# A two-layer decoder trunk on one core: search counts of ScalarE and filling matmuls laid out anew

## The chip, the core and the metric

The kernel runs on one core of a Trainium2 chip. The metric is the device time of one execution in microseconds (us). TensorE does the matmuls, VectorE, ScalarE and GpSimd the element-wise work, SyncE (the SP queue) issues the DMAs. Each engine runs its instructions in the order in which they are written, and waits on semaphores.

## The reference, cut to what matters

Input x is 1024 tokens by 1024 channels in float32. Layer 0 (even) projects x once and feeds two parallel head groups; layer 1 (odd) is a recurrent block that the change leaves alone.

```
proj = h @ even_w_in
score = sum over 8 index heads of w * relu(q_idx . k_idx), causal
_, idx = top_k(score, 256)                      # per query token
A: softmax over the 256 chosen keys (8 heads, relative bias) @ v, times silu(ag)
B: chunked gated linear attention, 4 heads, chunks of 64, head norm, times silu(bg)
x = x + rmsnorm(concat(A, B) @ even_w_out)
```

The 256 chosen keys of a token are found as a threshold on its score: a binary search over the 31 bits of a float, in which each trial counts how many scores lie above the candidate. Query blocks are 128 tokens; blocks 2 to 7 need the search. Block 7 has 1024 keys, block 6 has 896.

## The kernel before, in words

Every float32 product is made of three matmuls (high with high, high with low, low with high part of the operands), so each weight chunk is copied into a high part by ScalarE (`high(c)`) and a low part by GpSimd (`low(c)`), and each result that is used as an operand is split in the same way by ScalarE and VectorE.

**The search.** VectorE counts for blocks 2 to 5, all in one loop of 31 bits. For blocks 7 and 6 (`SIGNED = [7, 6]`, so b = 0 is block 7 and b = 1 is block 6) ScalarE counts: `sum_signs` (L950 to L964) takes the sign of score minus candidate over the row and sums it; `settle_signs` (L660 to L678) on GpSimd turns the count into the next candidate. Each block needs 32 such counts, one after the other. The 64 counts are placed by hand beside other work: `SIGNS_VALUE` in the 24 value tiles (products of 128 tokens by 256 channels for v of both groups), `SIGNS_KEYS` in the eight half-products of queries and keys of group B, `SIGNS_GATES` in the 16 half-products of the gates. In the gates loop ScalarE copies the half-product out (`gst`), takes its sigmoid (`g_sig`), in odd half-products makes `high` of a coming chunk, then runs `keys_out` (`kn`) and `gla_result` of linear attention, and last the counts. Half-products are numbered 0 to 15. TensorE runs, after half-product i, pieces of linear attention: `gla_turn`, `gla_update`, `gla_output`. `gla_output` waits for the `kn` copies of every turn so far, since both use one bank of PSUM; in half-products 4, 9 and 11 a turn stands directly ahead of an output.

**The masks.** After its loop VectorE fixes the ties of blocks 6 and 7 (`settle_ties`), makes the masks of blocks 2 to 7 (`make_mask`), and between them does `gla_mask` and `gla_state` for linear attention.

**Attention.** It runs in steps a = 0 to 33: 4 pairs of heads by 8 query blocks, so step 8p + q does pair p and block q. In step a TensorE does the logits of a (`head_logits`), then, for step a-1, in groups of up to four key blocks: it transposes the probabilities (`turn`), waits until ScalarE has copied them out (`pT`, L1103), and multiplies with v (`weigh`, L1981). Blocks 4 to 7 have two groups. Between the two, quarter pieces of the projections of the pairs (`pair_part`, 6 matmuls each, products (p, f) with f = 0 to 3, four pieces to a product) fill TensorE. `FILLERS` says how many pieces a step has. A finished product is split by ScalarE (`split_pair`, L1086) at the start of the next step, and by VectorE (`low_pair_result`, L1486), after which the next product may start. `head_logits` of a pair's first block waits until products (p, 0) and (p, 1) are split. VectorE adds the mask and bias to the logits (`masked`, L1498, both heads of the pair), which GpSimd prepares (`near_bias`, L770), and ScalarE takes the exponential (`exponent`, L1092). `head_logits` also waits for `masked` of the step before. In steps 4 to 7 GpSimd scales the results of group B, two tiles a step, each pair of tiles loaded and stored by SP in turn.

**The way out.** The output weights (8 chunks `C_WOE` + k) overwrite the projection's input, so `high` of them waits for the last pair product; one chunk a step in steps 26 to 33. SP loads a chunk when the one two before it has its low part. In SP's order the gates of group B (`mixT<-gate_d`, `load_b_gate`) stand among these loads; `gate_b` on VectorE multiplies them in steps 28 to 32, and TensorE's `turn_gla` waits for that.

Of the kernel before, what the change touches and what calls it, by code (L numbers as in the profile page):

```python
# [26 lines left out]
NT = T // P  # L27
KD = D // P
# [20 lines left out]
SIGNED = [7, 6]  # L49
# [36 lines left out]
def build(nc, x, rel_bias, pre_norm, post_norm, even_w_in, even_gate_w2, gate_b2, even_w_out,  # L86
# [185 lines left out]
    C_AV, C_BV, C_BQK, C_AG, C_BG, C_PAIR, C_WOE, C_ODD, C_WOO = 4, 8, 12, 16, 20, 24, 32, 40, 56  # L272
# [50 lines left out]
        return turned, turned + 1, min(turned + 3, 15)  # L323

    SUMMED_BESIDE, DECAYED_BESIDE = (30, 37), (37, 42)
    MASK_BESIDE = (46, 49, 55)
    STATE_BESIDE = (49, 51, 57)
    SIGNS_VALUE = [2, 1] * (3 * NT // 2)
    SIGNS_KEYS = [2, 1, 2, 1, 2, 1, 2, 1]
    SIGNS_GATES = [2] * 6 + [1] * 4 + [0] * 6  # L330

    INDEXED = []
    for n in range(len(QBS) * PAIRS):
# [8 lines left out]
    w_hi, w_lo = sem("w_hi"), sem("w_lo")  # L342
# [99 lines left out]

    parts = [(p, f, part) for p in range(PAIRS) for f in range(4) for part in range(4)][8:]
    FILLERS, ended = [], {}
    for a, count in enumerate([4, 4, 2, 2, 2, 2, 0, 0] * 3 + [4, 4]):
        FILLERS.append(parts[:count])
        for p, f, part in parts[:count]:
            ended[p, f] = a
        parts = parts[count:]

    def filler(a):

# [182 lines left out]
    def _(pool):  # L635
# [17 lines left out]
        settles, steps = itertools.count(), Tally(settle_step)  # L653
# [5 lines left out]

        def settle_signs():  # L660

            j, b = divmod(next(settles), len(SIGNED))
            w, col = (SIGNED[b] + 1) * P, slice(BY_COUNT + b, BY_COUNT + b + 1)
            up_f, up_i, tried_b = bit_up_f[:, b, :], bit_up_i[:, b, :], tried[:, b:b + 1]
            pool.wait_ge(signs_summed[b], j + 1)
            if j == 0:
                pool.wait_ge(bits_made, BITS + 1)
                own(pool.tensor_scalar(rej[:, col], cnt[:, col], float(w - 2 * TOPK + 1), None, ALU.is_gt))
                own(pool.tensor_scalar(side[:, b:b + 1], rej[:, col], -2.0, 1.0, ALU.mult, ALU.add))
                own(pool.tensor_tensor(up_f, bit_f[:, :], side[:, b:b + 1].to_broadcast([P, BITS + 1]), ALU.mult))  # L670
                own(pool.tensor_copy(up_i, up_f))
                pool.tensor_tensor(cand[:, col], up_i[:, 0:1], rej[:, col], ALU.subtract).then_inc(bit_settled[b], 1)  # L672
            else:
                own(pool.tensor_scalar(rej[:, col], cnt[:, col], float(w - 2 * TOPK + 1), up_f[:, j - 1:j], ALU.is_gt, ALU.mult))
# [42 lines left out]
        for i in range(3):  # L717
            for c in (8 + 2 * i, 9 + 2 * i):
                low(c)
            for t in range(NT):  # L720
                for n in range(SIGNS_VALUE[i * NT + t]):
                    settle_signs()

        pool.wait_ge(proj_full, nth_product("bqk", BQK_ORDER[0], 0))
        pool.memset(tri_f[:, :], 0.0).then_inc(pool_step, 1)
# [18 lines left out]
        for i in range(KD):  # L744
            for hf in range(2):
                pool.wait_ge(proj_copied, copy_count("g", C_AG + i, hf))
                pool.tensor_tensor(gst[:, hf, :], gst[:, hf, :], g_sig[:, :], ALU.mult).then_inc(silu_done, 1)
                if hf:
                    low(C_AG + 2 + i)
                for m in range(SIGNS_GATES[2 * i + hf]):  # L750
                    settle_signs()

        def scale_gla(t):
# [28 lines left out]
        for a in range(NW + 2):  # L782
            if a < NW:
                near_bias(a, 1)
            if a + 1 < NW:
                near_first(a + 1)
            if 4 <= a < 8:
                for t in range(2):
                    scale_gla(2 * (a - 4) + t)
            for p in range(1, PAIRS):  # L790
                for j in range(2):
                    if a == ended[p - 1, 2 + j] + 1:
                        low(C_PAIR + 2 * p + j)
            if 26 <= a < 34:
                low(C_WOE + a - 26)
        for t in range(1, NT):
            if t == 2:
                low(C_ODD)
# [22 lines left out]
    def _(act):  # L821
# [128 lines left out]
        def sum_signs():  # L950

            s = next(sums)
            j, b = divmod(s, len(SIGNED))
            qb, col = SIGNED[b], slice(BY_COUNT + b, BY_COUNT + b + 1)
            if s == 0:
                act.wait_ge(cand_zero, 1)
            else:
                act.wait_ge(signs_summed[(s - 1) % len(SIGNED)], (s - 1) // len(SIGNED) + 1)
# [16 lines left out]
            high(c)  # L975
        for t in range(NT):
            values_out("av", 1, t)
            for n in range(SIGNS_VALUE[t]):
                sum_signs()
        for c in (10, 11):  # L980
            high(c)
        for t in range(NT):
            values_out("bv", 0, t)
            for n in range(SIGNS_VALUE[NT + t]):
                sum_signs()
        for c in (12, 13):
            high(c)
        for pr, g_l in ((0, g_a), (1, kdec[:, 1, :])):
# [5 lines left out]
        for t in range(NT):  # L994
            values_out("bv", 1, t)
            if t == 0:
                own(act.activation(g_n0[:, :], g_a[:, :], ACT.Abs))
            if t == 1:
                own(act.activation(g_n1[:, :], kdec[:, 1, :], ACT.Abs))
            if t == 2:  # L1000
                own(act.activation(g_n0[:, :], g_n0[:, :], ACT.Exp, scale=-1.0))
            if t == 3:
                own(act.activation(g_n1[:, :], g_n1[:, :], ACT.Exp, scale=-1.0))
            if t == 4:
                act.activation(g_n0[:, :], g_n0[:, :], ACT.Ln, bias=onet).then_inc(ln_ready, 1)
            if t == 5:
                act.activation(g_n1[:, :], g_n1[:, :], ACT.Ln, bias=onet).then_inc(ln_ready, 1)
            for n in range(SIGNS_VALUE[2 * NT + t]):
                sum_signs()

        def exponents(pr):
            if pr:
# [37 lines left out]
        for i in range(16):  # L1050
            c, hf = C_AG + i // 2, i % 2
            q = nth_product("g", c, hf)
            act.wait_ge(proj_full, q + 1)
            if c > C_AG:
                act.wait_ge(gate_out[hf], 16 * (c - C_AG))
            act.activation(gst[:, hf, :], ps[:, q % 2, :], ACT.Copy)
            if i:
                act.wait_ge(silu_done, i)
            else:
                act.wait_ge(decs_ready, 2)  # L1060
            act.activation(g_sig[:, :], ps[:, q % 2, :], ACT.Sigmoid).then_inc(proj_copied, 1)
            if hf:
                high(c + 2)
            for t in range(NT):
                if i == gla_at(t)[0]:
                    keys_out(t)
            for t in range(NT):
                if i == gla_at(t)[2]:
                    gla_result(t)
            for m in range(SIGNS_GATES[i]):  # L1070
                sum_signs()
        act.wait_ge(o_out, NT)
        act.activation(grms, gssq, ACT.Sqrt, bias=epst, scale=1.0 / B_VAL).then_inc(gla_root, 1)
# [33 lines left out]
        for a in range(NW + 2):  # L1107
            for p, f in ended:
                if ended[p, f] == a - 1:
                    split_pair(p, f)  # L1110
            if 26 <= a < 34:
                high(C_WOE + a - 26)
            groups = blocks_of[a - 1] if 1 <= a <= NW else []
            for i in range(2):
                for g in groups[i:i + 1]:
# [161 lines left out]
    def _(dve):  # L1277
# [50 lines left out]
        n = 0  # L1328
# [205 lines left out]
            dve.wait_ge(b_turned, i + 1)  # L1534
            dve.tensor_tensor(mixT[:, KD // 2 + j, cols], ps[:, 0, :], mixT[:, KD // 2 + j, cols], ALU.mult).then_inc(b_gated, 1)

        gla_mask(3)
        make_mask(2)
        gla_state(3)
        make_mask(3)  # L1540
        gla_mask(4)
        make_mask(4)
        gla_state(4)
        gla_mask(5)
        make_mask(5)
        gla_state(5)
        settle_ties(1)
        make_mask(6)
        gla_mask(6)
        gla_state(6)  # L1550
        settle_ties(0)
        gla_mask(7)
        make_mask(7)
        gla_state(7)
        for f in range(2):
            low_pair_result(0, f)
        for a in range(NW + 3):
# [163 lines left out]
    def _(pe):  # L1721
# [298 lines left out]
                turn_gla(pieces_at(a)[1])  # L2020

        pe.wait_ge(out_done, NW)
        pe.wait_ge(w_lo, C_ODD)

        def out_tile(t, s, mh, ml, woh, wol, lo_done, freed, full):

            if isinstance(t, int) and t == 0:
                pe.wait_ge(ms_first, 1)
            else:
                pe.wait_ge(lo_done, t)  # L2030
            if freed is not None:
                pe.wait_ge(freed, t - 1)
            for hf in range(2):
                cols = slice(hf * HALF, (hf + 1) * HALF)
                for k in range(KD):
                    last = three(ps[:, S_BANK[s] + hf, :], (mh[:, s, k, :], ml[:, s, k, :]), (woh[:, k, cols], wol[:, k, cols]), k, KD)
            last.then_inc(full, 1)

# [141 lines left out]
```

## Time and profile before

| | |
|---|---|
| median of 3 runs | 1041.27 us (1038.85 to 1043.87) |
| profiled execution | 1043.11 us, span 1041.3 us, mean granted clock 0.982 |
| TensorE busy | 982.8 us, 94% of the span |
| VectorE, ScalarE, GpSimd busy | 630.5, 525.8, 331.2 us |
| value tiles / gates / attention | about 150 to 229 / 270 to 390 / 406 to 628 us |

The span is the trace's length; the profiled execution's own time lies 1.8 us above it. Busy time of TensorE includes matmuls that take twice as long at the lower clock. "Idle before" in a row is the time for which the engine stood still ahead of it, and the name behind the arrow is what ended that.

### The profile page before, as it was taken

To read this page: it belongs to the slowest core of one execution; us is meant where nothing else is said; L and a number is where in the kernel's file an instruction comes from. 1 tells how busy PE (TensorE), PEld (TensorE's weight loads), DVE (VectorE), ACT (ScalarE), POOL (GpSimd) and SP (SyncE) were. 2 spreads that over 40 slices of the span, in tenths; PEclk is the share of its full clock that TensorE was granted. 3 is DMA by queue.
4 is the path that set the end of the run, shared out by engine and by line. 5 is a ranking of instruction groups with operands and counts; after the bars stand their busy time and mean duration, and the time that the engine had idled before them with its cause. 6 is when DMAs were issued, how large, how long until landed. Compare 5 with 4: busy or idle time off the path is not lost.

```text
span 1041.3 us, 15136 instructions
## 1 busy us (share of the span) xinstructions
PE 982.8 (94%) x5706; PEld 799.6 (77%) x5706; DVE 630.5 (61%) x1080; ACT 525.8 (50%) x907; POOL 331.2 (32%) x428
## 2 busy tenths in 40 slices
PE   4998999999999899989999888999999999999997
PEld 3887789988877677767676666888888888888885
DVE  5312889959969781445444562665539394889252
ACT  6423677886755334544545463433437272766221
POOL 1310216546645422433131454110412222215200
PEclk8998999999999999999999998999999999999999
DMA  8243102201223323331010444221321111103152
GB/s 258 61 60 63 42 1 62 61 2 29 65 70 101 92 71 101 104 132 51 12 52 31 142 148 146 101 101 60 101 61 42 50 52 41 47 26 104 47 202 81
DMA packets 73919, 80.06 MB, mean 77 GB/s; under 512 B 5192, under 2 KB 58488, under 8 KB 73848
## 3 DMA queue, kind: packets, MB, share of 16 engines
q1 hardware_dynamic: 72576, 77.49, 23.7%
q10 hardware_dynamic: 1272, 1.62, 1.3%
q8 instruction: 44, 0.72, 0.3%
q14 instruction: 27, 0.22, 0.1%
HBM read 60.23 MB, written 18.35 MB: 75 GB/s over the span
## 4 chain that ended last, share of the span: by engine, by line
PE 67%; DVE 3%; ACT 3%; issue 2%; DMA 2%; POOL 1%; ACTq 0%; POOLq 0%; DVEq 0%
PE ps L1732 19%; PE ps L1734 19%; PE ps L1733 19%; PE ps L1981 3%; PE ps L1965 2%; PE ps L1917 1%; ACT pT L1103 1%; PE ps L1824 1%; DMA g_two<-gla_d 1%; ACT qkH L1086 1%; DVE qkL L1486 1%; PE ps L1912 1%; DMA gla_d<-g_two 1%; PE ps L2044 1%; PE ps L1825 1%
## 5 line engine op out<-in xcount | busy, mean ns | idle before, releaser
L1732 PE MATMUL ps<-hH,wH 128*128 128x512 f32 x384 | 157.3, 410 | 4.5 <-DVE qkL L1486 4.5
L1733 PE MATMUL ps<-hL,wH 128*128 128x512 f32 x384 | 151.2, 394 | 0.0
L1734 PE MATMUL ps<-hH,wL 128*128 128x512 f32 x384 | 151.1, 394 | 0.0
L1732 PE MATMUL ps<-h1H,w_slot_H 128*128 128x512 f32 x256 | 99.9, 390 | 0.0
L1734 PE MATMUL ps<-h1H,w_slot_L 128*128 128x512 f32 x256 | 99.8, 390 | 0.0
L1733 PE MATMUL ps<-h1L,w_slot_H 128*128 128x512 f32 x256 | 99.7, 390 | 0.0
L650 POOL TENSOR_TENSOR wL<-raw,wH 128x1024 fp32r<-128x1024 f32 x32 | 79.3, 2483 | 63.9 <-ACT wH L846 63.4
L1350 DVE TENSOR_SCALAR_CACHE_REDUCE junk<-score,cand 128x768 bf16<-128x768 f32 (+3 forms) x128 | 96.6, 809 | 1.1
L1732 PEld LDWEIGHTS ps<-hH,wH 128*128 128x128 f32 x384 | 73.0, 190 | 23.7 <-issue 9.9
L1734 PEld LDWEIGHTS ps<-hH,wL 128*128 128x128 f32 x384 | 72.9, 190 | 15.8
L1733 PEld LDWEIGHTS ps<-hL,wH 128*128 128x128 f32 x384 | 73.2, 191 | 13.2
L647 POOL TENSOR_TENSOR w_slot_L<-raw,w_slot_H 128x1024 fp32r<-128x1024 f32 x16 | 41.3, 2582 | 125.0 <-ACT w_slot_H L842 125.0
L1732 PE MATMUL ps<-wH,hH 128*128 128x256 f32 x256 | 76.1, 297 | 2.0 <-ACT bv L946 1.8
L963 ACT ACTIVATE signs<-score,cand 128x1024 bf16<-128x1024 f32 x64 | 70.1, 1095 | 7.1 <-POOL cand L672 4.1
L1733 PE MATMUL ps<-wL,hH 128*128 128x256 f32 x256 | 73.1, 286 | 0.0
L1734 PE MATMUL ps<-wH,hL 128*128 128x256 f32 x256 | 73.0, 285 | 0.0
L1103 ACT ACTIVATE pT<-ps 128x512 f32<-128x512 f32 (+3 forms) x96 | 41.9, 488 | 51.8 <-PE ps L1965 51.8
L1092 ACT ACTIVATE prob<-prob,small 128x128 f32<-128x128 f32 (+7 forms) x64 | 49.7, 777 | 30.1 <-DVE small L1504 30.1
L1498 DVE CUSTOM_DVE_ANT_0 prob<-ps,score 128x384 f32<-128x384 f32 (+5 forms) x48 | 42.7, 890 | 29.9 <-POOL score L770 20.0
L1732 PEld LDWEIGHTS ps<-wH,hH 128*128 128x128 f32 x256 | 49.6, 194 | 10.5 <-issue 10.5
L1734 PEld LDWEIGHTS ps<-h1H,w_slot_L 128*128 128x128 f32 x256 | 48.1, 188 | 10.0
L1733 PEld LDWEIGHTS ps<-h1L,w_slot_H 128*128 128x128 f32 x256 | 48.1, 188 | 9.9
(269 smaller groups left out, 2306.1 us busy)
## 6 DMA issues: line engine op xcount, KB each, us to landing
raw<-in_even_w_in SPq DMA_DIRECT2D x32, 512.0 KB, 4.2
xt<-in_x SPq DMA_DIRECT2D x16, 512.0 KB, 6.5
raw<-in_odd_w_in SPq DMA_DIRECT2D x16, 512.0 KB, 3.9
gate_d<-gst SPq DMA_DIRECT2D x16, 256.0 KB, 2.3
raw_row<-in_even_w_out SPq DMA_DIRECT2D x8, 512.0 KB, 3.3
x_d<-xt SPq DMA_DIRECT2D x8, 512.0 KB, 2.6
raw_row<-in_odd_w_out SPq DMA_DIRECT2D x8, 512.0 KB, 3.2
xt<-x_d SPq DMA_DIRECT2D x8, 512.0 KB, 4.8
```

What stands on the lines that cost most here:

```text
L647: pool.tensor_tensor(w_slot_L[s][:, :, :], raw[:, c % 2, :, :], w_slot_H[s][:, :, :].bitcast(F32), ALU.subtract).then_inc(w_lo, 1)
L650: pool.tensor_tensor(wL[:, s, :, :], raw[:, c % 2, :, :], wH[:, s, :, :].bitcast(F32), ALU.subtract).then_inc(w_lo, 1)
L963: act.activation(signs[:, 0:(qb + 1) * P], score_of(qb), ACT.Sign, bias=cand[:, col].bitcast(F32), scale=-1.0, accum_out=cnt[:, col]).then ...
L1092: act.activation(prob[:, i, 0:w], prob[:, i, 0:w], ACT.Exp, bias=nmx[:, c:c + 1], accum_out=lsum[:, c:c + 1]).then_inc(exp_done[e], 1)
L1103: act.activation(pT[:, e, 0:m * P], ps[:, TURN_BANK[e], 0:m * P], ACT.Copy).then_inc(turn_out, 1)
L1350: return steps(dve.tensor_scalar(junk1[:, j % 2, 0:(qb + 1) * P], score_of(qb), threshold, None, op, ALU.add, accum_out=dst[:, j:j + 1]))
L1498: dve.tensor_tensor_reduce(out=prob[:, i, 0:w].rearrange("p (b w) -> p b w", b=banks), in0=ps[:, b:b + banks, 0:wb], in1=mask_of(qb).rearr ...
L1732: pe.matmul(dst, lH, rH, start=k == 0, stop=False)
L1733: pe.matmul(dst, lH, rL, start=False, stop=False)
L1734: return pe.matmul(dst, lL, rH, start=False, stop=k == nk - 1)
L1965: last = pe.transpose(ps[:, TURN_BANK[e], i * P:(i + 1) * P], prob[:, buffer_of(n, e), (first + i) * P:(first + i + 1) * P], ident[:, :])
L1981: both = [pe.matmul(ps[e * A_DIM:(e + 1) * A_DIM, 7, 0:P], v[:, kb, (2 * p + e) * A_DIM:(2 * p + e + 1) * A_DIM], pT[:, e, i * P:(i + 1) * ...
```

## The change

It moves work and takes none away. Value tiles have one count each, all of block 6. The keys have eight counts of block 6 and four of block 7. The gates have two counts of block 7 in each of half-products 0 to 13, the first directly behind the sigmoid and the second where all stood before. The 16 filling pieces of a pair lie in eight steps. The low parts of the output weights come a step later, two of them in step 32, and TensorE waits for them one at a time. On VectorE one `gla_mask` moves into the search loop, and the ties of block 6 come first, those of block 7 last.

```diff
-    MASK_BESIDE = (46, 49, 55)
+    MASK_BESIDE = (46, 49, 55, 59)
-    SIGNS_VALUE = [2, 1] * (3 * NT // 2)
-    SIGNS_KEYS = [2, 1, 2, 1, 2, 1, 2, 1]
-    SIGNS_GATES = [2] * 6 + [1] * 4 + [0] * 6
+    SIGNS_KEYS = [2, 1] * 4
+    SIGNS_GATES = [2] * 14 + [0] * 2
+    SIGN_ORDER = [1] * (3 * NT) + [1, 0, 1] * 4 + [0] * 28
...
-    for a, count in enumerate([4, 4, 2, 2, 2, 2, 0, 0] * 3 + [4, 4]):
+    for a, count in enumerate([4, 4, 2, 2, 1, 1, 1, 1] + [1, 3, 4, 2, 2, 2, 1, 1] * 2 + [1, 3, 4]):
...
+    WOE_STEP = (27, 28, 29, 30, 31, 32, 32, 33)
...
             act.activation(g_sig[:, :], ps[:, q % 2, :], ACT.Sigmoid).then_inc(proj_copied, 1)
+            if SIGNS_GATES[i] > 1:
+                sum_signs()
             if hf:
                 high(c + 2)
...
-            for m in range(SIGNS_GATES[i]):
+            if SIGNS_GATES[i]:
                 sum_signs()
...
-            if 26 <= a < 34:
-                high(C_WOE + a - 26)
+            for k in range(KD):
+                if a == WOE_STEP[k]:
+                    high(C_WOE + k)
...
-        gla_mask(3)
+        gla_state(3)
         make_mask(2)
-        gla_state(3)
+        settle_ties(1)
+        gla_mask(4)
         make_mask(3)
-        gla_mask(4)
         make_mask(4)
...
-        settle_ties(1)
         make_mask(6)
         gla_mask(6)
         gla_state(6)
+        gla_mask(7)
+        gla_state(7)
         settle_ties(0)
-        gla_mask(7)
         make_mask(7)
-        gla_state(7)
...
-        pe.wait_ge(w_lo, C_ODD)
...
+                    if isinstance(t, int) and t == 0 and hf == 0:
+                        pe.wait_ge(w_lo, C_WOE + k + 1)
```

**Place 1: ScalarE, gate half-product 11.** Before, `g_sig` is followed by the high part of a weight chunk, the copy `kn`, and the results of linear attention:

```order
L1056 ACTIVATE gst<-ps 128x512
L1061 ACTIVATE g_sig<-ps 128x512
L846 ACTIVATE wH<-raw 128x1024
L1035 ACTIVATE kn<-ps 128x256
L1043 ACTIVATE g_st<-ps 128x2x2x128
```

In the changed kernel, whose lines are numbered a few higher:

```order
L1060 ACTIVATE gst<-ps 128x512
L1065 ACTIVATE g_sig<-ps 128x512
L970 ACTIVATE signs,cnt<-score,cand 128x1024
L852 ACTIVATE wH<-raw 128x1024
L1039 ACTIVATE kn<-ps 128x256
L1047 ACTIVATE g_st<-ps 128x2x2x128
```

A count over 1024 keys now stands between `g_sig` and `kn`; so it does in half-products 4 and 9.

**Place 2: ScalarE, steps 7 and 8 of attention.** Before, the exponential of block 7's second head (128x1024) is followed by the copies of the next transposes; the split of a pair product (`qkH`) comes only after step 8:

```order
L1103 ACTIVATE pT<-ps 128x384 x2
L1092 ACTIVATE prob,small<-prob,small 128x1024
L1103 ACTIVATE pT<-ps 128x512 x2
L1092 ACTIVATE prob,small<-prob,small 128x128
L1103 ACTIVATE pT<-ps 128x512 x2
L1092 ACTIVATE prob,small<-prob,small 128x128
L1086 ACTIVATE qkH_118<-ps 128x512
```

Changed:

```order
L1109 ACTIVATE pT<-ps 128x384 x2
L1098 ACTIVATE prob,small<-prob,small 128x1024
L1092 ACTIVATE qkH_118<-ps 128x512
L1109 ACTIVATE pT<-ps 128x512 x2
L1098 ACTIVATE prob,small<-prob,small 128x128
```

The split of product (1, 1), which was done in step 6, stands directly behind that exponential, and the logits of step 8 need its result.

**Place 3: ScalarE, steps 26 to 28.** Before, the first output chunk (`woH`) comes in step 26, whose `pT` copies have 256 columns:

```order
L1086 ACTIVATE qkH_118<-ps 128x512
L829 ACTIVATE woH<-raw_row 128x1024
L1103 ACTIVATE pT<-ps 128x256 x2
L1092 ACTIVATE prob,small<-prob,small 128x384 x2
L829 ACTIVATE woH<-raw_row 128x1024
L1103 ACTIVATE pT<-ps 128x384 x2
```

Changed:

```order
L1109 ACTIVATE pT<-ps 128x256 x2
L1098 ACTIVATE prob,small<-prob,small 128x384 x2
L1092 ACTIVATE qkH_118<-ps 128x512
L835 ACTIVATE woH<-raw_row 128x1024
L1109 ACTIVATE pT<-ps 128x384 x2
L1098 ACTIVATE prob,small<-prob,small 128x512 x2
```

The last pair product and the first output chunk both moved one step later; GpSimd's `woL` moved with them, and SP's loads wait for `woL`.

## Rows read from the trace of the kernel before

**Rows 1.** The page, part 5: value tiles; last, idle before, releaser

```profile
L1732 PE MATMUL ps<-wH,hH 128*128 128x256 f32 x256 | 76.1, 297 | 2.0 <-ACT bv L946 1.8
```

**Rows 2.** The view of waits, TensorE alone: us in total, times, longest

```profile
PE ps L1981 <- ACT pT L1103: 10.9, 20, 0.7
```

**Rows 3.** Timeline of ScalarE, half-products 0 and 11 of the gates: start, us

```profile
277.59 1.14 ACT L963 ACTIVATE signs<-score,cand 128x1024 bf16<-128x1024 f32 x1
...
278.86 1.04 ACT L963 ACTIVATE signs<-score,cand 128x896 bf16<-128x896 f32 x1
...
355.55 0.59 ACT L1061 ACTIVATE g_sig<-ps 128x512 f32<-128x512 f32 x1
...
356.97 0.39 ACT L1035 ACTIVATE kn<-ps 128x256 f32<-128x256 f32 x1
```

**Rows 4.** Timeline of TensorE, first row after each wait for kn

```profile
302.09 0.45 PE L1912 MATMUL ps<-state,bqk 64*64 64x128 f32 x8 [0.68 <-ACT kn L1035]
...
341.19 0.45 PE L1912 MATMUL ps<-state,bqk 64*64 64x128 f32 x8 [0.85 <-ACT kn L1035]
...
357.61 0.45 PE L1912 MATMUL ps<-state,bqk 64*64 64x128 f32 x8 [1.73 <-ACT kn L1035]
```

**Rows 5.** Stretches: busy time of each engine, granted clock, DMA share, GB/s

```profile
355.00:360.00 5.00, 3.27 (x36) 2.48 (x34) 0.00 (x0) 2.30 (x4) 3.57 (x2) 0.93 0.29 79
360.00:365.00 5.00, 5.00 (x18) 4.01 (x17) 4.55 (x14) 1.63 (x9) 0.00 (x0) 0.73 0.44 135
400.00:405.00 5.00, 3.50 (x16) 2.61 (x15) 0.69 (x1) 0.60 (x1) 0.00 (x0) 1.00 0.21 81
```

**Rows 6.** Chain that ended last, steps 7 to 9: start, us, what

```profile
455.91 0.02 ACT prob L1092
...
457.86 0.23 PE ps L1732
...
466.81 0.61 ACT qkH L1086
...
468.28 0.47 PE ps L1732
```

**Rows 7.** Timeline of TensorE: second pair product; logits of step 8

```profile
403.67 0.47 PE L1732 MATMUL ps<-hH,wH 128*128 128x512 f32 x1 [1.50 <-DVE qkL L1486]
...
455.83 0.39 PE L1824 MATMUL ps<-qkH 64*128 64x256 f32 x2 [0.76 <-DVE small L1498]
```

**Rows 8.** Timeline of TensorE in steps 14 to 16

```profile
502.04 0.33 PE L1981 MATMUL ps<-pT,v 128*64 128x128 f32 x2 [0.63 <-ACT pT L1103]
...
504.84 0.50 PE L1824 MATMUL ps<-qkH 64*128 64x512 f32 x2
...
511.60 0.39 PE L1824 MATMUL ps<-qkH 64*128 64x256 f32 x2
```

**Rows 9.** Timeline of ScalarE, last exponential of step 15

```profile
510.63 1.15 ACT L1092 ACTIVATE prob<-prob,small 128x1024 f32<-128x1024 f32 x1
```

**Rows 10.** Timeline of TensorE, logits of steps 27 and 28

```profile
589.32 0.50 PE L1824 MATMUL ps<-qkH 64*128 64x512 f32 x2 [1.00 <-DVE small L1498]
...
593.92 0.42 PE L1824 MATMUL ps<-qkH 64*128 64x320 f32 x2 [1.18 <-DVE small L1498]
```

**Rows 11.** Timeline of GpSimd, low part of the first output chunk

```profile
589.07 2.38 POOL L641 TENSOR_TENSOR woL<-raw_row,woH 128x1024 fp32r<-128x1024 f32 x1
```

**Rows 12.** Timeline of the SP queue, steps 26 to 28

```profile
585.52 0.93 SPq L577 DMA_DIRECT2D g_back<-gla_d  x2
...
595.93 0.33 SPq L473 DMA_DIRECT2D raw_row<-in_even_w_out  x1
...
596.78 0.91 SPq L538 DMA_DIRECT2D mixT<-gate_d  x2
```

**Rows 13.** Timeline of VectorE: a gate of group B; step 32

```profile
602.50 0.69 DVE L1535 TENSOR_TENSOR mixT<-ps,mixT 128x512 f32<-128x512 f32 x1 [0.83 <-DMA mixT<-gate_d]
...
619.89 2.15 DVE L1511 COPY rl<-small 128x128 f32<-128x128 f32 x1
```

More of the change, by code:

```diff
@@ L660, in settle_signs @@
         def settle_signs():
-            j, b = divmod(next(settles), len(SIGNED))
+            s = next(settles)
+            b = SIGN_ORDER[s]
+            j = SIGN_ORDER[:s].count(b)
             w, col = (SIGNED[b] + 1) * P, slice(BY_COUNT + b, BY_COUNT + b + 1)
@@ L720, in _ @@
             for t in range(NT):
-                for n in range(SIGNS_VALUE[i * NT + t]):
-                    settle_signs()
+                settle_signs()
         pool.wait_ge(proj_full, nth_product("bqk", BQK_ORDER[0], 0))
@@ L747, in _ @@
                 pool.tensor_tensor(gst[:, hf, :], gst[:, hf, :], g_sig[:, :], ALU.mult).then_inc(silu_done, 1)
+                if SIGNS_GATES[2 * i + hf] > 1:
+                    settle_signs()
                 if hf:
                     low(C_AG + 2 + i)
-                for m in range(SIGNS_GATES[2 * i + hf]):
+                if SIGNS_GATES[2 * i + hf]:
                     settle_signs()
@@ L793, in _ @@
                         low(C_PAIR + 2 * p + j)
-            if 26 <= a < 34:
-                low(C_WOE + a - 26)
+            for k in range(KD):
+                if a == WOE_STEP[k]:
+                    low(C_WOE + k)
         for t in range(1, NT):
@@ L952, in sum_signs @@
             s = next(sums)
-            j, b = divmod(s, len(SIGNED))
+            b = SIGN_ORDER[s]
+            j = SIGN_ORDER[:s].count(b)
             qb, col = SIGNED[b], slice(BY_COUNT + b, BY_COUNT + b + 1)
@@ L957, in sum_signs @@
             else:
-                act.wait_ge(signs_summed[(s - 1) % len(SIGNED)], (s - 1) // len(SIGNED) + 1)
+                act.wait_ge(signs_summed[SIGN_ORDER[s - 1]], SIGN_ORDER[:s].count(SIGN_ORDER[s - 1]))
             if j == 0:
@@ L977, in _ @@
             values_out("av", 1, t)
-            for n in range(SIGNS_VALUE[t]):
-                sum_signs()
+            sum_signs()
         for c in (10, 11):
@@ L983, in _ @@
             values_out("bv", 0, t)
-            for n in range(SIGNS_VALUE[NT + t]):
-                sum_signs()
+            sum_signs()
         for c in (12, 13):
@@ L1007, in _ @@
                 act.activation(g_n1[:, :], g_n1[:, :], ACT.Ln, bias=onet).then_inc(ln_ready, 1)
-            for n in range(SIGNS_VALUE[2 * NT + t]):
-                sum_signs()
+            sum_signs()
         def exponents(pr):
@@ L1061, in _ @@
             act.activation(g_sig[:, :], ps[:, q % 2, :], ACT.Sigmoid).then_inc(proj_copied, 1)
+            if SIGNS_GATES[i] > 1:
+                sum_signs()
             if hf:
@@ L1110, in _ @@
                     split_pair(p, f)
-            if 26 <= a < 34:
-                high(C_WOE + a - 26)
+            for k in range(KD):
+                if a == WOE_STEP[k]:
+                    high(C_WOE + k)
             groups = blocks_of[a - 1] if 1 <= a <= NW else []
```

## The prediction, made before the changed kernel ran

> **What bounds the kernel now.** I read the page first, then TensorE's waits, then the timelines around each of them. TensorE is busy for 94% of the span and the chain that ended last runs mostly through it, so the change counts only where TensorE begins to wait or stops waiting. Its waits where the change works are few: 2.0 us in the value tiles [rows 1], 0.68, 0.85 and 1.73 in three places for `kn` [rows 4], and 10.9 us for the `pT` copies of ScalarE [rows 2]. The reader should see in them that there is little to win, and that ScalarE, busy for half of the span, is waited for at moments, not on average: the place of an instruction in its queue matters more than its sum.
>
> **Value tiles.** 24 counts instead of 36, all of the narrower block. With 12 counts fewer ScalarE releases the banks in time, and the 2.0 us fall away [rows 1]. It can't be more, for there is no other wait. The 12 counts go to the gates. Sum so far **-2.0**.
>
> **Gates.** A count of 1024 keys followed by another instruction takes 278.86 - 277.59 = 1.27 us of ScalarE's queue [rows 3]. In half-product 11 the sigmoid begins at 355.55 and `kn` at 356.97 [rows 3], and TensorE, which has nothing else to do, goes on at 357.61 after 1.73 us [rows 4]. The new count stands between the two. The same holds in half-products 4 and 9 (0.68 and 0.85). So each wait grows by 1.27, to 1.95, 2.12 and 3.0: 3 x 1.27 = **+3.8**. In the other half-products a whole product of over 6 us lies between the copy and its use, and covers it. The second count behind the results has the rest of the half-product as its cover, also in 10 to 13. The search of block 7 now ends in half-product 13, not 9; its ties and mask (3.9 and about 9.3 us on VectorE, estimated from the instructions of before) then end some 2 us before VectorE is needed for the first pair product. I cost that at nothing; without this cover each us late is a us.
>
> **Filling in steps 4 to 9.** Steps 6 and 7 get a piece, and a piece between transposes and `weigh` hides 0.63 us. But the pieces only pay where TensorE sets the pace: in steps 4 to 7 GpSimd's scaling of group B, chained through DMAs, holds back the masks, and step 7's second exponential still begins at 455.91 [rows 6]. Behind it now stands the split of product (1, 1). The exponential takes about 1.2, then come split, VectorE's part and TensorE's start, which the rows put at 468.28 - 466.81 = 1.47 [rows 6]. The logits of step 8 thus start at 455.91 + 1.2 + 1.47 = 458.6, where they started at 455.83 [rows 7]: +2.8. The second group of step 8 loses its piece (+0.63), a wait of 0.16 ends, and in step 9 the wait of 0.59 for the split (468.28 less TensorE's last end) ends since its product goes on. 2.8 + 0.63 - 0.16 - 0.59 = **+2.7**.
>
> **Steps 14 to 17 and 22 to 25.** Steps 14 and 15 win a gap of 0.63 each [rows 8]. A piece costs six matmuls at 0.23 = 1.4 us wherever it stands [rows 6]. In step 15 the last exponential began 5.8 us after the logits (510.63 - 504.84) [rows 8, 9]; the piece puts the second transposes 0.7 later, so 6.5. Exponential 1.2 and the 1.47 bring the logits of step 16 to 9.2 us after those of step 15. TensorE's own work would bring them to 6.8 (511.60 - 504.84) + 1.4 - 0.6 = 7.5 [rows 8]. Wait 1.7. Per pair: -1.26 + 1.7 + 0.63 - 0.59 = +0.5; twice: **+1.1** with rounding.
>
> **Steps 26 to 28.** The last product (3, 3), four pieces, now fills step 26, which was short and made step 27 wait 1.00 [rows 10]. From the end of the last piece (585.4; the load that it releases goes out at 585.52 [rows 12]) to the logits of step 28 (593.92) passed 8.5 us, of which I count 3.2 as waits. After: step 26's own 2.4 and a wait of 0.2, then from the end of the pieces 4.2 to the logits of step 28 (split, VectorE, first mask, GpSimd's bias, second mask): 6.8. **-1.7**.
>
> **Steps 28 to 30.** Of the moved step everything counts. The first output chunk's low part ended at 589.07 + 2.38 = 591.45 [rows 11], and SP then loaded the third chunk and a gate; at 595.93 the fourth chunk, and behind it at 596.78 the gates that `gate_b` of step 29 needs [rows 12]. One landed at 602.50, and VectorE had waited 0.83 for it [rows 13]: no slack. Each is queued behind a low part that now comes one step later. A step there is 593.92 - 589.32 = 4.6 us [rows 10]. Behind VectorE's `gate_b` stand the masks, hence the logits of step 30, and TensorE's own transposes of group B. 4.6 less 0.6 that I estimate TensorE has to spare: **+4.0**. If it were wholly hidden it would be 0, and as VectorE was already waiting I take the upper end.
>
> **Step 32.** Two chunks in one step put a second high part (about 1 us) ahead of `pT`, after waiting for its load; but VectorE's copy for the inverses is late there anyway (2.15 us where 0.23 is usual) [rows 13] and covers most. **+0.7**. Waiting per chunk for the output weights wins nothing: the last low part is done a us before the first product's operand.
>
> The stalls sum to -2.0 + 3.8 + 2.7 + 1.1 - 1.7 + 4.0 + 0.7 = **+8.6**.
>
> **The clock.** After the wait of 1.73 us at half-product 11 the granted clock was 0.93 and 0.73 of 2.4 GHz for five us each, that is partly at 1.2 GHz: 5 x 0.07 + 5 x 0.27 = 1.7 us lost [rows 5]. After a wait of 1.50 us at 403.67 it stayed at 1.00 [rows 5, 7]. New waits longer than 1.73: 1.95 and 2.12 in the gates, 3.4 ahead of step 8, up to 2.7 in step 29. I count three at 1.7: **+5.1** (none: 0; all, with steps 16 and 24: 6 x 1.7 = 10.2). The Trainium skill, TensorE: Matmul & The Clock Gate (Part 1), says that how many matmuls run slow varies from run to run, and for modelling puts the penalty below 1% of a typical span and advises against fitting it. By that the term would be left out and the result would be the rival of 1050 below.
>
> 8.6 + 5.1 = 13.7. The profiled execution took 1043.1, its span 1041.3 equals the median 1041.27; on the median that gives **1055.0 us**.
>
> **Rivals.**
> - *The clock doesn't fall at the new waits*: only 8.6, 1049.9 us. For it: the rows have 1.73 with and 1.50 without a fall, and nothing says that 1.95 elsewhere must act like 1.73.
> - *The gates of group B land in time*: the DMAs find the queues emptier, and steps 28 to 30 cost nothing, with the clock as before: 8.6 - 4.0 = 4.6, 1045.9 us, no change. Against it: 0.83 was waited before [rows 13]. It decides if a transfer takes under 2 us where 5.7 (602.50 - 596.78) was seen.
> - *Filling wins everywhere* (the faster side): if the products of steps 7, 15 and 23 were split before TensorE gets to the next logits, pieces would cover all waits in attention that they can reach: six of 0.63, three of 0.59 and 3.8 in steps 26 to 28, 9.4 us, with steps 28 to 30 covered too: -9.4 - 2.0 + 3.8 = -7.6, 1033.7 us. It decides at 7.5 us after the logits of step 15; I get 9.2. For it speaks only that ScalarE is half idle.
>
> **Chances.** Forecast 0.50, clock unmoved 0.30, gates in time 0.12, filling wins 0.08. 0.5% is 5.2 us, about what the measurement can tell. Slower 0.80, same 0.12, faster 0.08. Range: from 1046 (the third case) to 1062 (stalls 8.6, clock 10.2, and 2 for noise); it leaves out the last case and the ends.
>
> **What would show it.** TensorE's wait for `kn` at about 7 us in three places, not 3.3; waits ahead of the logits of steps 8, 16 and 24 of about 3.4, 1.7 and 1.7, released by `qkL`; two or three new stretches below 1.00 in the granted clock in the gates and in attention; VectorE waiting 2 to 5 us for `mixT<-gate_d`; the waits for `pT` down from 10.9 to about 9; none in the value tiles. I am wrong if `kn` isn't what TensorE waits for, or if step 7 is no longer held by GpSimd, or if a mask or the search of block 7 comes late ahead of the first step, which would cost more than I say.

## The result and the profile after

The changed kernel takes 1054.33 us (median of 4 runs, 1053.16 to 1055.03), beside 1042.55 us for the kernel before on the same chip (4 runs). The ratio is 1.0122, with a 95% interval of 1.0100 to 1.0143: slower by 1.2%, as forecast (1055.0). The forecast stood on 1041.27 us for the kernel before, so the rise that it named was 13.7 us, and the rise measured is 11.8. The profiled execution took 1053.16 us with a span of 1051.4, 10.1 more than the span of before.

I read the page first: TensorE's busy sum moved only from 982.8 to 985.6 us, so most of the time had to be in waits. Here are TensorE's waits in the changed kernel (releaser, us in total, times, longest); `pT` answers to [rows 2], `kn` to [rows 4]:

```profile
PE ps L1987 <- ACT pT L1109: 9.9, 18, 0.7
...
PE ps L1918 <- ACT kn L1039: 7.4, 3, 3.3
PE ps L1830 <- DVE qkL L1493: 6.6, 3, 3.6
...
PE ps L2000 <- DVE mixT L1542: 4.1, 2, 2.8
...
PE ps L1979 <- DVE rl L1518: 2.2, 1, 2.2
```

`kn` went from 3.3 to 7.4, in the same three places. `qkL` ahead of logits (L1830) and `mixT` are new. `pT` fell only from 10.9 to 9.9. I then went to each place, beginning in the value tiles. From 150 to 232 us TensorE's timeline has one wait left, where before it had three of 0.18, 0.34 and 1.43 us:

```profile
162.45 0.36 PE L1738 MATMUL ps<-wH,hH 128*128 128x256 f32 x1 [0.35 <-ACT v L952]
```

**Gates.** ScalarE's timeline at half-product 11, to be laid beside [rows 3]; the first row is the second count of half-product 10:

```profile
356.06 1.15 ACT L970 ACTIVATE signs<-score,cand 128x1024 bf16<-128x1024 f32 x1 [3.35 <-POOL cand L679]
...
357.21 0.57 ACT L1060 ACTIVATE gst<-ps 128x512 f32<-128x512 f32 x1
357.69 0.58 ACT L1065 ACTIVATE g_sig<-ps 128x512 f32<-128x512 f32 x1
358.16 1.14 ACT L970 ACTIVATE signs<-score,cand 128x1024 bf16<-128x1024 f32 x1
359.20 0.20 ACT L970 ACTIVATION_READ_ACCUMULATOR signs<-score,cand 128x1 f32 x1
359.30 1.05 ACT L852 ACTIVATE wH<-raw 128x1024 fp32r<-128x1024 f32 x1
360.24 0.38 ACT L1039 ACTIVATE kn<-ps 128x256 f32<-128x256 f32 x1
```

And TensorE's timeline at the three copies of `kn`, for [rows 4]:

```profile
301.14 0.69 PE L1918 MATMUL ps<-state,bqk 64*64 64x128 f32 x8 [1.80 <-ACT kn L1039]
...
342.88 0.45 PE L1918 MATMUL ps<-state,bqk 64*64 64x128 f32 x8 [2.26 <-ACT kn L1039]
...
360.87 0.45 PE L1918 MATMUL ps<-state,bqk 64*64 64x128 f32 x8 [3.29 <-ACT kn L1039]
```

The count stands between sigmoid and `kn`, which now begins 2.55 us after the sigmoid (360.24 - 357.69) where it was 1.42 [rows 3]. The waits grew by 1.12, 1.41 and 1.56. The count itself makes 1.13 to 1.14 us of each. At half-product 9 the remaining 0.28 is TensorE's own: it arrives that much earlier, since a wait of 0.21 us for VectorE (at 339.02 us in the trace of before) is gone. At half-product 11 the remaining 0.43 comes from the second count of half-product 10: it had waited 3.35 us for GpSimd's candidate, and so the copy `gst` began 0.65 us after TensorE's transposes (357.21 - 356.56), where it was 0.20 before (355.06 - 354.86).

**Attention.** ScalarE's timeline in step 7 (the exponential, then the split) and TensorE's ahead of the logits of steps 8, 16 and 24; step 8 began at 455.83 before and step 16 at 511.60 [rows 7, 8]:

```profile
458.44 1.15 ACT L1098 ACTIVATE prob<-prob,small 128x1024 f32<-128x1024 f32 x1 [2.07 <-DVE small L1511]
459.49 0.19 ACT L1098 ACTIVATION_READ_ACCUMULATOR prob<-prob,small 128x1 f32 x1
459.59 0.58 ACT L1092 ACTIVATE qkH<-ps 128x512 fp32r<-128x512 f32 x1
```

```profile
460.94 0.39 PE L1830 MATMUL ps<-qkH 64*128 64x256 f32 x2 [3.64 <-DVE qkL L1493]
...
517.88 0.39 PE L1830 MATMUL ps<-qkH 64*128 64x256 f32 x2 [1.46 <-DVE qkL L1493]
...
573.21 0.39 PE L1830 MATMUL ps<-qkH 64*128 64x256 f32 x2 [1.46 <-DVE qkL L1493]
```

The split waits in ScalarE's queue behind an exponential that is itself late, and TensorE waits for split and VectorE's low part. What makes it late is still GpSimd, as the prediction had it: the mask of step 7's second head waited for it, here 4.10 us, while GpSimd waited 5.20 us for the load of group B's results.

```profile
456.98 1.23 DVE L1505 CUSTOM_DVE_ANT_0 prob<-ps,score 128x1024 f32<-128x1024 f32 x1 [4.10 <-POOL score L775]
```

**Steps 28 to 30.** SP's timeline (issues to its queue), VectorE's copies into `mixT`, and TensorE's transposes of group B; of before see [rows 12, 13]:

```profile
600.24 0.35 SPq L475 DMA_DIRECT2D raw_row<-in_even_w_out  x1
600.63 0.43 SPq L540 DMA_DIRECT2D mixT<-gate_d  x1
604.86 0.33 SPq L475 DMA_DIRECT2D raw_row<-in_even_w_out  x1
605.24 0.68 SPq L537 DMA_DIRECT2D a_gate<-gate_d  x1
605.96 0.91 SPq L540 DMA_DIRECT2D mixT<-gate_d  x2
```

```profile
605.74 0.69 DVE L1542 TENSOR_TENSOR mixT<-ps,mixT 128x512 f32<-128x512 f32 x1 [2.15 <-DMA mixT<-gate_d]
...
611.72 0.69 DVE L1542 TENSOR_TENSOR mixT<-ps,mixT 128x512 f32<-128x512 f32 x1 [3.88 <-DMA mixT<-gate_d]
```

```profile
606.58 0.63 PE L2000 MATMUL ps<-ident,g_back 128*128 128x128 f32 x4 [1.26 <-DVE mixT L1542]
...
612.56 1.08 PE L2000 MATMUL ps<-ident,g_back 128*128 128x128 f32 x4 [2.84 <-DVE mixT L1542]
```

The gates at 605.96 leave right behind the fourth chunk at 604.86, which waited for GpSimd: SP's wait from 600 to 615 us is 13.5 us, all for `woL`. They left at 596.78 before.

**Stage by stage.** The stages are cut where TensorE or ScalarE begins the same thing in both traces: ScalarE's first gate copy, TensorE's logits of a step, its first product of the output (641.04 us, 631.25 before). The stage from the first gate copy to step 0 is called the gates below. The table gives each stage's length and, in it, the time for which TensorE stood still; the last column is the change of that idle time.

| stage | length before, changed | idle before, changed | change of idle |
|---|---|---|---|
| 150 us to first gate copy | 125.20, 123.12 | 1.95, 0.35 | -1.6 |
| to step 0 | 131.39, 136.78 | 4.97, 8.86 | +3.9 |
| steps 0 to 4 | 22.44, 22.46 | 0.79, 0.80 | 0.0 |
| steps 4 to 12 | 56.60, 56.64 | 4.13, 6.16 | +2.0 |
| steps 12 to 20 | 55.40, 55.34 | 3.21, 3.57 | +0.4 |
| steps 20 to 28 | 52.89, 53.88 | 6.23, 4.78 | -1.5 |
| steps 28 to 30 | 11.01, 15.35 | 1.36, 5.03 | +3.7 |
| step 30 to first output product | 26.32, 27.47 | 7.93, 8.29 | +0.4 |

In all TensorE's idle time grows from 30.6 to 37.8 us, by 7.2, and the kernels are 9.8 us apart at the first output product; the other 2.5 us are busy time of TensorE.

### The profile page after: what moved, and what is told of

Read it like the earlier page. It is cut to its first block, busy times and chain, and to the rows that moved or that the text cites. A ratio compares the mean times of both kernels' runs of the same rounds, so it can differ in the third digit from the quotient of the medians.

```text
span 1051.4 us, 15135 instructions
## 1 busy us (share of the span) xinstructions
PE 985.6 (94%) x5706; PEld 802.8 (76%) x5706; DVE 625.7 (60%) x1080; ACT 525.6 (50%) x907; POOL 335.9 (32%) x428
## 4 chain that ended last, share of the span: by engine, by line
PE 82%; DVE 5%; ACT 4%; DMA 3%; issue 2%; POOL 2%; SPq 0%; ACTq 0%; DVEq 0%; POOLq 0%
PE ps L1738 24%; PE ps L1739 22%; PE ps L1740 22%; PE ps L1987 3%; PE ps L1971 2%; PE ps L1830 2%; PE ps L1832 1%; PE ps L1831 1%; PE ps L1923 1%; DMA g_two<-gla_d 1%; DVE score L1344 1%; PE ps L1787 1%; DVE qkL L1493 1%; PE ps L1918 1%; ACT relu L945 1%
## 5 line engine op out<-in xcount | busy, mean ns | idle before, releaser
L1738 PEld LDWEIGHTS ps<-hH,wH 128*128 128x128 f32 x384 | 73.4, 191 | 21.4 <-issue 7.4
L970 ACT ACTIVATE signs<-score,cand 128x896 bf16<-128x896 f32 (+1 forms) x64 | 70.1, 1096 | 16.1 <-POOL cand L679 11.7
L775 POOL TENSOR_TENSOR score<-nearm,near 128x256 f32<-128x256 bf16 x48 | 31.9, 677 | 82.1 <-DVE small L1505 81.6
L1740 PEld LDWEIGHTS ps<-h1H,w_slot_L 128*128 128x128 f32 x256 | 48.1, 188 | 10.1
```

The costliest lines, as they stand in the source:

```text
L775: pool.tensor_tensor(dst, nearm[:, qb, NEAR - w:NEAR], near[:, p % 2 * 2 + e, NEAR - w:NEAR], ALU.add).then_inc(near_ready, 1)
L1738: pe.matmul(dst, lH, rH, start=k == 0, stop=False)
L1740: return pe.matmul(dst, lL, rH, start=False, stop=k == nk - 1)
```

## The experiments

Each is compared with the kernel before on its own chip, where that took 1041.48 us (the first four) or 1041.27 us (the others), and not the 1042.55 us beside which the changed kernel stands. Where a version is compared with the changed kernel, two differences are therefore given: of the medians, and of the distances from the kernel before. Where no interval is given, the number is from one profiled execution. "Step n" is TensorE's beginning of the logits of step n.

### The two halves of the change

**Counts only**: the changed table of counts and VectorE's order, with the fillers, output chunks and TensorE's single wait for them as before.

```diff
-    for a, count in enumerate([4, 4, 2, 2, 1, 1, 1, 1] + [1, 3, 4, 2, 2, 2, 1, 1] * 2 + [1, 3, 4]):
+    for a, count in enumerate([4, 4, 2, 2, 2, 2, 0, 0] * 3 + [4, 4]):
...
-    WOE_STEP = (27, 28, 29, 30, 31, 32, 32, 33)
+    WOE_STEP = (26, 27, 28, 29, 30, 31, 32, 33)
...
```

> The counts, the gates' order and VectorE's mask order of the changed kernel; filling pieces, output weights and their wait as before. My theory: value tiles give 2 us back, three waits for kn grow by 1.27 each and the clock falls at two more places, so +3 to +5.5 on the kernel before (about 1046 to 1048), the kn waits are 1.8, 2.3 and 3.3 us as in the changed kernel, and steps 6, 7, 26 and 27 look as before. Rival (filling and output weights carry nothing, all of the loss is the counts): about 1054. Rival (the extra 12 counts of ScalarE in the gates are hidden): 1040 to 1042.

Measured: 1048.21 us, ratio 1.0067 (1.0043 to 1.0091), +6.7, a little over the 3 to 5.5 expected. The waits for `kn` are 7.0 in all. Step 0 is 6.6 later than before, and from there to the first output product nothing is lost (224.3 us, 224.7 before).

**Filling only**: before with the new fillers, output steps and waits per chunk.

```diff
-    for a, count in enumerate([4, 4, 2, 2, 2, 2, 0, 0] * 3 + [4, 4]):
+    for a, count in enumerate([4, 4, 2, 2, 1, 1, 1, 1] + [1, 3, 4, 2, 2, 2, 1, 1] * 2 + [1, 3, 4]):
...
+    WOE_STEP = (27, 28, 29, 30, 31, 32, 32, 33)
...
```

> Filling pieces, output weights and their waits of the changed kernel; counts and VectorE's order as before. My theory: waits of 3.6, 1.5 and 1.5 us ahead of the logits of steps 8, 16 and 24 and a VectorE wait for the gates of group B in step 29, together with a fall of the clock +6 to +8.5 (about 1049 to 1051). The two halves e1 and e2 should add up to the changed kernel's +11.8 within 1.5 us. Rival (counts carry the loss): 1042. Rival (filling pays when the gates stage is left alone): below 1042.

Measured: 1050.79 us, ratio 1.0089 (1.0076 to 1.0102), +9.3, over the 6 to 8.5 expected. Its waits of TensorE:

```profile
PE ps L1828 <- DVE qkL L1490: 6.5, 3, 3.6
...
PE ps L1998 <- DVE mixT L1539: 3.3, 2, 1.9
PE ps L1916 <- ACT kn L1038: 3.3, 3, 1.7
```

`qkL` and `mixT` come with the filling, `kn` with the counts: both halves lose, each by its own waits. Together they lose less (11.8) than apart (6.7 + 9.3), by 4.3 us where 1.5 at most was expected. Part of that can be the clock, below: the gates of the version with counts only took 140.9 us in its trace, 4.1 more than the 136.8 of the changed kernel's, with the same instructions. More than that isn't shown.

### One wait each

**`kn` first**: in the changed kernel, the first count of a half-product moves behind the copy of `kn` and ahead of the results.

```diff
-            if SIGNS_GATES[i] > 1:
-                sum_signs()
             if hf:
                 high(c + 2)
...
+            if SIGNS_GATES[i] > 1:
+                sum_signs()
```

> The changed kernel with the first count of each gate half-product moved behind the copy kn (still ahead of the results of linear attention); the number of counts is the same. My theory (place, not amount): the waits for kn go back to 0.7, 0.85 and 1.7, 3.8 us of waits and up to 3.4 us of slow clock go, 1047 to 1050.5. Rival (ScalarE has too much to do in the gates): no change, 1053 to 1055. If only the waits matter and the clock doesn't, 1050.5; if the clock counts in full, 1047.

Measured: 1050.25 us, ratio 1.0086 (1.0071 to 1.0101), 4.1 less than the changed kernel's 1054.33, and 3.0 less by the distances from before. TensorE's waits and ScalarE's timeline at half-product 11:

```profile
PE ps L1918 <- ACT kn L1039: 3.8, 3, 2.0
```

```profile
354.36 0.58 ACT L1065 ACTIVATE g_sig<-ps 128x512 f32<-128x512 f32 x1
354.83 1.05 ACT L852 ACTIVATE wH<-raw 128x1024 fp32r<-128x1024 f32 x1
355.78 0.38 ACT L1039 ACTIVATE kn<-ps 128x256 f32<-128x256 f32 x1
356.04 1.15 ACT L970 ACTIVATE signs<-score,cand 128x1024 bf16<-128x1024 f32 x1
```

Sigmoid to `kn` is 1.42 us again, and the wait there is 2.0; the 0.27 over the 1.73 of before come from a second count of half-product 10 ahead of `gst`, as above. The gates take 131.7 us, as before (131.4), where they took 136.8 in the changed kernel. Step 0 is 1.2 us earlier than before, though the gates hold the same 28 counts as in the changed kernel: their number costs little, the place of one in each half-product did. The medians alone put the gain at 3 to 4 us, with intervals that touch; the waits (7.4 to 3.8) carry the reading.

**Gates early**: in the changed kernel, the loads of all four gates of group B are issued on SP where the first one was, ahead of the output chunks.

```diff
-        load_b_gate(0)
+        for j in range(KD // 2):
+            load_b_gate(j)
...
-        load_b_gate(1)
...
```

> The changed kernel with all four gate loads of group B issued at once where the first stood, ahead of the loads of output weights, instead of between them. My theory (the gates are queued behind loads that wait for a low part one step later): VectorE's waits for mixT and TensorE's 1.3 and 2.8 us in step 29 vanish, 4 to 6 us, 1048.5 to 1050.5. Rival (the DMA rings are what is full, the gates would be late anyhow, or the earlier loads push the chunk loads back): within 1 us of the changed kernel.

Measured: 1049.99 us, ratio 1.0080 (1.0058 to 1.0101), 4.3 less (3.3 by the distances). No wait for `mixT` is left, and step 28 to step 30 takes 10.7 us, where the changed kernel takes 15.35 and before 11.0.

**The same edit on the kernel before**:

> The kernel before with all four gate loads of group B issued at once where the first stood. VectorE waited only 0.8 us for one of them there, off TensorE's path for the most part. My theory: -1 to +0.5 us. Rival (the loads order hurt the kernel before as well): -3 us or more.

Measured: 1041.43 us, ratio 1.0000 (0.9985 to 1.0015). There the queueing was on the edge, as 0.83 us of VectorE's wait said [rows 13], and off TensorE's path. So the move of the chunks by one step made it a cost, and the early load mends only that.

**Pieces ahead**: the changed kernel with one filling piece moved from step 9 (17, 25) to step 6 (14, 22), so that product (1, 1) and its like end and are split one step earlier.

```diff
-    for a, count in enumerate([4, 4, 2, 2, 1, 1, 1, 1] + [1, 3, 4, 2, 2, 2, 1, 1] * 2 + [1, 3, 4]):
+    for a, count in enumerate([4, 4, 2, 2, 1, 1, 2, 1] + [1, 2, 4, 2, 2, 2, 2, 1] * 2 + [1, 2, 4]):
```

> The changed kernel with FILLERS = [4,4,2,2,1,1,2,1] + [1,2,4,2,2,2,2,1]*2 + [1,2,4]: the same number of pieces in all, but products (1,1), (2,1) and (3,1) end in steps 6, 14 and 22, and steps 7, 15 and 23 begin the next product. My theory (the logits of a pair's first block wait for a split queued behind the last exponential): the waits of 3.6, 1.5 and 1.5 ahead of the logits of steps 8, 16 and 24 fall to the 0.8 of the kernel before or to nothing; 5 to 6 us of waits go and one fall of the clock may go with them; 1047.5 to 1050. Rival (these logits wait for the masks anyway): above 1053.

Measured: 1045.47 us, ratio 1.0046 (1.0029 to 1.0063), 8.9 less (7.6 by the distances), more than the 4 to 7 expected. ScalarE's timeline in steps 6 and 7:

```profile
449.56 1.04 ACT L1098 ACTIVATE prob<-prob,small 128x896 f32<-128x896 f32 x1 [0.15 <-DVE small L1511]
450.51 0.19 ACT L1098 ACTIVATION_READ_ACCUMULATOR prob<-prob,small 128x1 f32 x1
450.60 0.58 ACT L1092 ACTIVATE qkH<-ps 128x512 fp32r<-128x512 f32 x1
```

The split is over before the last exponentials of block 7. The three waits of 6.6 us in all are gone, and `pT` is down from 9.9 to 8.3. Steps 4 to 28 take 9.2 us less than in the changed kernel's trace (156.67 instead of 165.86), 5.0 of them in steps 4 to 12; there the fall of the clock after the wait of 3.64 us is gone as well.

### The three together

**All three** edits on the changed kernel.

> The changed kernel with three edits at once: first count of a gate half-product behind the copy kn, the gates of group B loaded at once, pieces one step ahead as in e5. My theory: the three sources are separate, so their parts add: 4 + 4.3 + 5 off 1054.3, and with value tiles and filled gaps left as gains it ends at 1039 to 1042, at or below the kernel before. Rival (the sources share one cause, such as a clock that falls wherever TensorE first waits): 1045 or more.

Measured: 1032.88 us, ratio 0.9916 (0.9901 to 0.9930): 8.4 us below the kernel before, and well below the 1039 to 1042 expected. It is 21.4 below the changed kernel, where the parts sum to 4.1 + 4.3 + 8.9 = 17.3 (20.2 and 13.9 by the distances). Its waits of TensorE:

```profile
PE ps L1985 <- ACT pT L1107: 8.4, 17, 0.7
...
PE ps L1916 <- ACT kn L1037: 3.8, 3, 2.0
```

In the traces nothing is left over: each stage takes what the single edit gave it. The gates take 131.65 us (`kn` first: 131.69), steps 4 to 12 take 51.78 (pieces ahead: 51.63), steps 12 to 20 and 20 to 28 take 53.26 and 51.77 (53.26 and 51.78), steps 28 to 30 take 10.69 (gates early: 10.68). What differs in the single versions is the gates, where the waits for `kn` still stood in two of them: 136.4 us in the trace with pieces ahead, 140.4 in the one with gates early. So the medians' excess of 4 to 6 us over the sum is most likely slow clock in the gates of the single versions; medians can't be split by stage, so this stays argued.

**Last chunk later**: all three edits, with the last three output chunks in steps 32, 33 and 33.

```diff
-    WOE_STEP = (27, 28, 29, 30, 31, 32, 32, 33)
+    WOE_STEP = (27, 28, 29, 30, 31, 32, 33, 33)
```

> e6 with the seventh chunk of the output weights prepared in step 33 and not in step 32 (WOE_STEP ends 31, 32, 33, 33). My theory: the second high part no longer stands ahead of the pT copies of step 32, 0.6 us off TensorE's wait there, and the per-chunk wait covers the later low parts; 0 to 1 us below e6. Rival: the last low parts come after their first use, 1 to 3 us above e6.

Measured: 1032.49 us, ratio 0.9917 (0.9900 to 0.9934), the same. With two chunks in step 32, TensorE waits for `pT` right behind its wait for VectorE's inverses, in the version above and, here, in the changed kernel:

```profile
632.80 0.33 PE L1979 MATMUL ps<-ident,rl 128*128 128x128 f32 x1 [2.24 <-DVE rl L1518]
...
633.69 1.09 PE L1987 MATMUL ps<-pT,v 128*64 128x128 f32 x16 [0.55 <-ACT pT L1109]
```

With the chunk moved this wait is gone, as in the kernel before, but TensorE then waits longer ahead of the first output product, 4.84 us instead of 3.40:

```profile
624.20 0.77 PE L1736 MATMUL ps<-woH,msH 128*128 128x512 f32 x1 [4.84 <-issue]
```

There the low parts of the last two chunks come one after the other on GpSimd, the second ending at 623.0 us (620.2 in the version above). So what is won in step 32 is lost again behind it: step 30 to the first output product takes 28.0 us, 26.7 in the version above.

### The clock

To see what of the clock belongs to the kernel, the changed kernel was profiled twice more and the kernel before once more.

> The changed kernel itself, profiled a second time, to see what of its clock falls belongs to the kernel. If a wait of TensorE of a given length always brings a fall, the falls stand where they stood: after 301, 361, 461, 612 and 641 us and not after 343, and 22.8 us are lost in all. If the falls after waits of one to three us are not fixed by the kernel, some of these places change, in steps of about 1.7 us, while the waits for kn, qkL and mixT stay within 0.5 us of 7.4, 6.6 and 4.1. I expect the second, since the version with the gates early, whose program is the same up to the gates, had falls after 343 too and stood 3.8 us later at step 0. Span 1048 to 1055.

> The same once more. Same waits within 0.5 us; clock falls at another choice of the same places, total lost 20 to 25 us; span 1048 to 1055.

> The kernel before, profiled a second time. The waits of TensorE for kn stay at 3.3 in all. If the falls are not fixed by the kernel, the one of 1.7 us after 357 may be missing or one after 302, 341 or 456 may be there; total lost 16 to 23 us, span 1038 to 1044. If they are fixed, 19.5 us are lost at the same places.

Measured: 1054.11, 1057.40 and 1043.27 us. The second changed trace has a span of 1055.6 us, a little above the 1048 to 1055 expected, and the second one of before lost 12.5 us to the slow clock in all, where 16 to 23 were expected. The waits for `kn`, `qkL` and `mixT` are the same to 0.5 us. TensorE waited 2.26 us for `kn` ahead of 343 us in each of the three traces of the changed kernel. Stretches of the first, second and third of them (stretch, length, busy us and instructions of PE, PEld, DVE, ACT and POOL, granted clock, DMA share, GB/s):

```profile
343.00:350.00 7.00, 7.00 (x47) 5.65 (x47) 6.77 (x9) 2.76 (x11) 4.42 (x5) 1.00 0.45 129
```

```profile
343.00:350.00 7.00, 7.00 (x41) 5.62 (x34) 6.77 (x9) 2.76 (x11) 4.11 (x5) 0.76 0.46 129
```

```profile
343.00:350.00 7.00, 6.46 (x32) 4.95 (x33) 6.83 (x7) 3.05 (x13) 4.12 (x3) 0.51 0.46 128
```

After the same wait the clock stayed at 2.4 GHz, lost 7 x 0.24 = 1.7 us, and lost 7 x 0.49 = 3.4. The Trainium skill, TensorE: Matmul & The Clock Gate (Part 1), says that the number of matmuls that run slow at a kernel's start varies from run to run. It says it of the start only; here the traces show the same behind a wait in the middle. Summed over the stretches of 1 us between 300 and 650 us, the loss is 11.9, 13.6 and 17.0 us in the three traces of the changed kernel and 6.8 and 5.1 in the two of before. In the changed kernel it fell in all three traces near 301, 363, 461, 612 and 640 us, the first four after waits of 1.8, 2.9 to 3.3, 3.6 and 2.8, and in none after the waits of 1.46 ahead of steps 16 and 24. Two places differed: 343, and 363, where the third trace lost 3.4 us and the others 1.7. Both are in the gates, and so is most of what separates the three traces: the gates took 136.8, 137.9 and 140.5 us, while from step 4 to step 30 no stage differs by more than 0.12 us.

## Why the prediction came out right

The prediction is right in direction and, term by term, in mechanism; that it ends 0.7 us from the median is in part luck. The rise is 11.8 us, not 13.7, and 1.3 of the difference is hidden because the kernel before took 1042.55 us here and not 1041.27.

**Right mechanism and size: the value tiles (-2.0).** ScalarE's first gate copy is 2.1 us earlier. TensorE's idle time falls by 1.6, and 0.35 us of wait is left there.

**Right mechanism, a little small: `kn` (+3.8).** The three waits grew by 4.1. A count cost 1.13 to 1.14 us at each place, not 1.27; what the second counts add at half-product 11 (0.43) was put at nothing. Moving the count alone brings the kernel back by 3.0 to 4.1 us.

**Right mechanism, a little large: steps 4 to 9 (+2.7).** The wait ahead of step 8 is 3.64 (said: 3.4), the split stands where I put it, and GpSimd still holds step 7. Step 4 to step 12 takes the same time as before with two pieces fewer, at 6 x 0.23 = 1.4 us each, so 2.8 are lost. But only 2.0 of them are idle time. The other 0.8 is busy time, and the fall of the clock at 461 lies there, which the prediction counts under the clock: with the same number of pieces and no fall, TensorE is busy there for 1.4 us less in the version with pieces ahead (49.10 instead of 50.48).

**Mis-sized: steps 14 to 17 and 22 to 25 (+0.5 a pair).** Step 12 to 20 takes 55.34 us (before 55.40), with the same number of pieces: -0.1, and its idle time grows by 0.4. The wait ahead of step 16 is 1.46, not 1.7, and the gaps filled cover it. Step 20 to 28 takes 1.0 more with two pieces more, so -1.8, of which -1.5 is idle time, where -1.7 for steps 26 to 28 and +0.5 for the pair were forecast; what of it lies in which is not separated. (Twice 0.48 is 1.0; the prediction adds 1.1.)

**Right: steps 28 to 30 (+4.0).** 15.35 instead of 11.01 us: +4.3, of which 3.7 is idle time. VectorE waited 2.15 and 3.88 us for the gates. The cause was tested by the early loads, on both kernels.

**Right mechanism, small: step 32 (+0.7).** The wait for `pT` behind the second chunk is 0.55 us. Idle time from step 30 to the first output product grows by 0.4, and the stretch by 1.2; the other 0.8 is busy time, more of it at the slow clock than before.

**The sum of stalls (+8.6)**: TensorE's idle time grew by 7.2. The forecast is too large by 0.7 in steps 4 to 12 and by 0.2 to 0.3 in each of the four stages behind them, and too small by 0.4 in the value tiles and 0.1 in the gates.

**The clock (+5.1)** was three falls of 1.7. New ones stand near 301, 461 and 612 us, the last of two steps, while the one of 1.7 at 622 us of before is gone, so three more. That the traces to be compared show just 11.9 - 6.8 = 5.1 us lost is luck: it is four new steps less an old one, and the other two traces of the changed kernel lost 13.6 and 17.0. Nor is all of it paid: TensorE's busy time up to the first output product grew by 2.5 us in this trace, 4.0 and 7.4 in the other two. Some 0.4 of the fall at 612 lies in the wait itself, where a slow clock costs nothing; where the rest goes is open. By the median the difference is 11.8 us, 4.6 over the idle time. So the term was right in kind, and in size within what executions differ by. Leaving it out gives 1050 us, 4 below the median. The prediction has the advice to do so from the Trainium skill, TensorE: Matmul & The Clock Gate (Part 1); what that passage puts below 1% is the slow start of a kernel, so it says nothing of falls behind a wait. That I named 343 us among the likely places shows the limit: it fell there in two traces of three.

**The rivals.** Clock unmoved (1049.9): the clock did fall more than before, in all three traces. Gates in time (1045.9): VectorE waited. Filling wins everywhere (1033.7): wrong for this table, as the split came too late; but with one piece a pair moved, the gates loaded early and `kn` first, 1032.9 is what is measured. That rival named its own condition rightly. That its 1033.7 is met is luck, though: it kept the 3.8 us of the waits for `kn`, which the version measured has not, and a version with pieces ahead and gates early alone wasn't run.

## What to carry to other kernels

Find the instruction that another engine waits for, and count what stands between its operand and it in its queue; a count of 1.1 us put there cost 1.1 us each time. Put right behind it, it cost TensorE at most 0.3 us at each of the three places, 0.5 in all. A filler that waits for another engine also delays what stands behind it in the queue, as the count of half-product 10 did. When a step is moved, follow every queue its DMAs pass: here a load queued behind a chunk on SP cost 3 to 4 us though nothing about it was changed. Even spreading of filler paid here only where each unit of it was finished a step before its result was needed: shifting one piece of sixteen turned a loss of 12 us into one of 4.

## What the runs showed of the hardware that was not expected

Falls of the clock come in steps of 1.7 us lost, and whether one comes after a wait of 1.0 to 2.3 us is not fixed by the kernel. 2.26 us gave none, one step and two in three executions of one program. 1.73 us gave one [rows 5] in both profiles of the kernel before, and none in the version with filling only (granted clock 1.00 from 357 to 364 us) nor in the kernel before with the gates early. Even the waits of 1.46 us, which brought no fall in the changed kernel, brought one in the version with filling only, ahead of step 24 (1.7 us lost from 569 to 573), and a wait of 1.00 us brought one at 587 us in the kernel before with the gates early.

```profile
568.57 0.39 PE L1828 MATMUL ps<-qkH 64*128 64x256 f32 x2 [1.46 <-DVE qkL L1490]
```

One profiled execution therefore can't place a term of 2 to 4 us. Nor is a fall always paid for: the two profiles of before lost 19.5 and 12.5 us in all, 5.1 of the difference between 17 and 29 us, yet step 0 begins at 406.6 and 407.1 us and the spans are 1041.3 and 1041.5. What would fix the falls was not found.
